# Query and key panels with the weight pieces stationary, and the row scale as a row

## The reference, cut to what matters

```python
hn   = rmsnorm(x, mixer_norm)                       # x * rsqrt(mean(x^2) + eps) * w, per token
proj = hn @ w_in                                    # (256, 2048) @ (2048, 6176)
q, k, v, og, lr = split(proj, 1024, 2048, 4096, 6144)
gk   = lr @ w_gate_up + b_gate                      # lr has rank 2 x 16
logdec = log_sigmoid(gk) / 16
o = gla(q / 16, k, v, logdec) in both directions    # needs q and k with channels down the partitions
o = rmsnorm(o) * silu(og);  x = x + o @ w_out
```

## Time and profile before

| | us |
|---|---|
| median of 3 runs | 1728.8 (1727.99 to 1729.51) |
| span of the profiled execution | 1727.2 |
| PE busy in it | 1705.6 |
| DVE, ACT, POOL busy | 1025.0, 802.1, 99.4 |

### The profile page before, as it was taken

One profiled execution on the slowest core, in us unless ns is written; L12 is line 12 of the kernel. 1 busy time (PEld: TensorE's weight loads), 2 busy tenths in 40 slices (PEclk: granted clock), 3 DMA queues, 4 the chain that ended last, 5 costly groups with the idle time before them and its releaser, 6 DMA issues.

```text
span 1727.2 us, 21748 instructions
## 1 busy us (share of the span) xinstructions
PE 1705.6 (99%) x7827; PEld 1401.8 (81%) x7827; DVE 1025.0 (59%) x1085; ACT 802.1 (46%) x967; POOL 99.4 (6%) x95
## 2 busy tenths in 40 slices
PE   8999999999999999999999999999999999999997
PEld 6888877888777888877888888888888888888886
DVE  4444465566755899955555455455465465565755
ACT  4444444444456555545444443443434444444653
POOL 6000000000110122210000000000000000000001
PEclk9999999999999999999999999999999999999999
DMA  8566645666464644555656566666566666656553
GB/s 258 158 188 184 183 146 147 219 209 215 149 199 134 177 147 152 157 165 180 218 183 190 188 192 191 188 190 191 189 189 191 190 188 192 191 187 194 180 184 133
DMA packets 160175, 315.46 MB, mean 183 GB/s; under 512 B 9772, under 2 KB 11888, under 8 KB 159216
## 3 DMA queue, kind: packets, MB, share of 16 engines
q1 hardware_dynamic: 158480, 304.12, 56.6%
q0 software_dynamic: 1632, 10.46, 1.6%
HBM read 310.36 MB, written 4.19 MB: 182 GB/s over the span
## 4 chain that ended last, share of the span: by engine, by line
PE 96%; DVE 2%; DMA 1%; ACT 1%; issue 0%; POOL 0%; POOLq 0%; DVEq 0%; SPq 0%; ACTq 0%
PE acc L588 29%; PE acc L590 29%; PE acc L589 29%; PE aux L604 2%; PE aux L745 2%; DMA w_raw<-in_w_out 1%; DVE w_lo L1248 1%; PE aux L811 0%; PE aux L637 0%; PE aux L758 0%; PE aux L759 0%; PE aux L636 0%; ACT w_hi L937 0%; DVE h_tok L1478 0%; PE aux L729 0%
## 5 line engine op out<-in xcount | busy, mean ns | idle before, releaser
L1248 DVE TENSOR_TENSOR w_lo<-w_raw,w_hi 128x1024 fp32r<-128x1024 f32 x572 | 704.9, 1236 | 584.7 <-ACT w_hi L937 584.1
L937 ACT CAST w_hi<-w_raw 128x1024 fp32r<-128x1024 f32 x572 | 599.9, 1051 | 821.3 <-PE acc L590 796.6
L588 PE MATMUL acc<-w_hi,a_hi 128*128 128x512 f32 x1664 | 658.6, 396 | 3.0 <-DVE w_lo L1248 3.0
L590 PE MATMUL acc<-w_hi,a_lo 128*128 128x512 f32 x1664 | 650.2, 391 | 0.0
L589 PE MATMUL acc<-w_lo,a_hi 128*128 128x512 f32 x1664 | 649.7, 390 | 0.0
L588 PEld LDWEIGHTS acc<-w_hi,a_hi 128*128 128x128 f32 x1664 | 313.7, 189 | 72.9 <-issue 10.3
L590 PEld LDWEIGHTS acc<-w_hi,a_lo 128*128 128x128 f32 x1664 | 313.4, 188 | 66.5
L589 PEld LDWEIGHTS acc<-w_lo,a_hi 128*128 128x128 f32 x1664 | 313.9, 189 | 62.8 <-issue 0.2
L588 PE MATMUL acc<-w_hi,act_hi 128*128 128x512 f32 x320 | 124.6, 389 | 0.0
L590 PE MATMUL acc<-w_hi,act_lo 128*128 128x512 f32 x320 | 124.5, 389 | 0.0
L589 PE MATMUL acc<-w_lo,act_hi 128*128 128x512 f32 x320 | 124.5, 389 | 0.0
(11 more groups left out here) (236 smaller groups left out, 887.9 us busy)
## 6 DMA issues: line engine op xcount, KB each, us to landing
w_raw<-in_ffn_w_in SPq DMA_DIRECT2D x176, 512.0 KB, 3.4
w_raw<-in_w_in SPq DMA_DIRECT2D x112, 512.0 KB, 3.6
w_raw<-in_gla_w_in SPq DMA_DIRECT2D x96, 512.0 KB, 3.9
w_raw<-in_ffn_w_out SPq DMA_DIRECT2D x88, 512.0 KB, 3.6
w_raw<-in_w_out SPq DMA_DIRECT2D x32, 512.0 KB, 4.7
w_raw<-in_gla_w_out SPq DMA_DIRECT2D x32, 512.0 KB, 3.6
w_raw<-in_ple_w_gate SPq DMA_DIRECT2D x32, 512.0 KB, 3.9
x_tok<-in_x SPq DMA_DIRECT2D x8, 256.0 KB, 8.7
```

The costliest lines, as they stand in the source:

```text
L588: pe.matmul(banks[t][:], hi[:, k + c, tok], wh, start=st, stop=False)
L590: mm = pe.matmul(banks[t][:], lo[:, k + c, tok], wh, start=False, stop=en)
L937: nc.scalar.copy(w_hi[u % RING][:], w_raw[u % RING][:]).then_inc(hi_done, 1)
L1248: nc.vector.tensor_tensor(w_lo[u % RING][:], w_raw[u % RING][:], w_hi[u % RING][:], ALU.subtract).then_inc(lo_done, 1)
```

## The change

In panels 0 to 3 the operands change places. `turned_unit` keeps a piece of the weights, 128 rows by 128 columns, stationary and moves the 256 tokens of `a_hi` or `a_lo` past it: 2 chunks x 4 column blocks x 3 = 24 matmuls of 256 columns. The panel then has output channels down the partitions, as `gqT` and `gkT` want it, so the eight `gt` jobs, the four `stage_panel` calls before them and ACT's copies go; DVE writes `gqT` and `gkT` from the panel's two banks (2 instructions of 128x512 at g = 9, 17, 25, 33).

Tokens now run along the free dimension, so the scale must be a row on all partitions. At g = 6 DVE spreads `rstd[1]` to two 128x128 tiles (`root_wide`), a new job `row` behind unit 7 turns them on PE against the identity (2 float32 matmuls), and ACT copies the result to `root_row` at g = 7. `lr_tok` and `lrt` go as well; DVE scales the rank product with `root_row` at g = 9. The rest of the kernel is the same. The diff, cut:

```diff
@@ gla_jobs
+    if g == 7:
+        found.append(("row", 0))
     if g == 8:
         found.append(("lr", 0))
-    if g in (9, 17, 25, 33):
-        p = (g - 9) // 8
-        found += [("gt", 2 * p), ("gt", 2 * p + 1)]
-    if g == 10:
-        found.append(("lr_tok", 0))
-    if g == 12:
-        found.append(("lrt", 0))
@@ POOL, before the first product with gkT
-                    for i in range(4, 8):
-                        job_read(pool, "gt", i)
+                    panel_read(pool, P_G + 3)
@@ PE
+            def turned_unit(u, p, hi, lo, k, first, last):
+
+                pe.wait_ge(lo_done, u + 1)
+                if first and p >= 2:
+                    panel_read(pe, p - 2)
+                banks = panel_banks(p)
+                for c in range(UNIT):
+                    st, en = first and c == 0, last and c == UNIT - 1
+                    for blk in range(N // P):
+                        half = blk % 2
+                        o = banks[blk // 2][:, half * TOK:(half + 1) * TOK]
+                        wh = w_hi[u % RING][:, c, blk * P:(blk + 1) * P]
+                        wl = w_lo[u % RING][:, c, blk * P:(blk + 1) * P]
+                        pe.matmul(o, wh, hi[:, k + c, :], start=st and half == 0, stop=False)
+                        pe.matmul(o, wh, lo[:, k + c, :], start=False, stop=False)
+                        mm = pe.matmul(o, wl, hi[:, k + c, :], start=False, stop=en and half == 1)
+                mm.then_inc(unit_used, 1)
-                unit(U_G + g, P_G + p, a_hi, a_lo, 2 * j, j == 0, j == UPP - 1)
+                shape = turned_unit if p < 4 else unit
+                shape(U_G + g, P_G + p, a_hi, a_lo, 2 * j, j == 0, j == UPP - 1)
...
+                    if name == "row":
+
+                        pe.wait_ge(root_spread, TT)
+                        b = begin("row")
                         for t in range(TT):
+                            mm = pe.matmul(b[:, t * P:(t + 1) * P], root_wide[:, t, :], ident[:], start=True, stop=True)
...
                     if name == "dg":
                         if i == 0:
-                            job_read(pe, "gt", 6)
-                            job_read(pe, "gt", 7)
+                            panel_read(pe, P_G + 3)
@@ ACT (the copies of lr, lr_tok, lrt and gt go too)
+                if g == 7:
+                    job_done(act, "row")
+                    nc.scalar.copy(root_row[:], bank_of("row")[:, 0:TOK]).then_inc(read_of("row"), 1)
...
-                    if p < 4:
+                    if 4 <= p < 8:
                         act.wait_ge(rstd_done, 2)
-                        stage_panel(P_G + p, og[p % 2], rstd[1])
@@ DVE, behind low(U_G + g + RING)
-                    nc.vector.memset(lrt[:, :, 2 * RANK:], 1.0).then_inc(zeros, 1)
+                    nc.vector.memset(lrT[2 * RANK:2 * RANK + 1, :], 1.0).then_inc(zeros, 1)
...
+                if g == 6:
+                    dve.wait_ge(rstd_done, 2)
+                    for t in range(TT):
+                        nc.vector.tensor_scalar(root_wide[:, t, :], ident[:], 0.0, rstd[1][:, t:t + 1], ALU.mult,
+                                                ALU.add).then_inc(root_spread, 1)
+                if g == 9:
+                    job_read(dve, "row")
+                    job_done(dve, "lr")
+                    nc.vector.tensor_tensor(lrT[0:2 * RANK, :], bank_of("lr")[0:2 * RANK, 0:TOK],
+                                            root_row[0:2 * RANK, :], ALU.mult).then_inc(read_of("lr"), 1)
+                if g in (9, 17, 25, 33):
+                    p = (g - 9) // 8
+                    panel_done(dve, P_G + p)
+                    row = root_row[:].rearrange("p (a t) -> p a t", a=1).broadcast_to([P, 2, TOK])
+                    for i, b in enumerate(panel_banks(P_G + p)):
+                        src = b[:].rearrange("p (k t) -> p k t", t=TOK)
+                        k = 4 * (p % 2) + 2 * i
+                        nc.vector.scalar_tensor_tensor((gqT if p < 2 else gkT)[:, k:k + 2, :], src,
+                                                       1.0 / 16.0 if p < 2 else 1.0, row, ALU.mult,
+                                                       ALU.mult).then_inc(acc_read[(P_G + p) % 2], 1)
```

More of the change, by code:

```diff
@@ L240, in block_kernel @@
     lr_lo = at("lr_lo", [P, KD, 2 * RANK], F32R, W + 60 * KB)
-    lrt = at("lrt", [P, TT, 2 * RANK + 1], F32, W + 64 * KB)
+    root_row = at("root_row", [P, TOK], F32, W + 62 * KB)
+    root_wide = at("root_wide", [P, TT, P], F32, W + 63 * KB)
     lrT = at("lrT", [2 * RANK + 1, TOK], F32, W + 64 * KB + 288)
@@ L324, in block_kernel @@
         fg_split, lr_split = sem("fg_split"), sem("lr_split")
+        root_spread = sem("root_spread")
         tanh_done = sem("tanh_done")
@@ L785, in _ @@
                         thin("lr", lr_hi, lr_lo, 2 * RANK)
[L786 to L793, removed]
-                        for t in range(TT):
[L795 to L802, removed]
+                    if name == "row":
+                        pe.wait_ge(root_spread, TT)
+                        b = begin("row")
+                        for t in range(TT):
+                            mm = pe.matmul(b[:, t * P:(t + 1) * P], root_wide[:, t, :], ident[:], start=True, stop=True)
                         mm.then_inc(aux_done, 1)
@@ L805, in _ @@
                         if i == 0:
-                            job_read(pe, "lrt")
+                            job_read(pe, "lr")
                             pe.wait_ge(up_in, 64)
@@ L1144, in _ @@
                 if j == UPP - 1:
-                    if p < 4:
+                    if 4 <= p < 8:
                         act.wait_ge(rstd_done, 2)
-                        stage_panel(P_G + p, og[p % 2], rstd[1])
-                    elif p < 8:
                         act.wait_ge(emb_out, 16)
                         stage_panel(P_G + p, gv[:, :, (p - 4) * N:(p - 3) * N], rstd[1])
-                    else:
+                    elif p >= 8:
                         if p >= 10:
@@ L1529, in times @@
                 if s == 0:
-                    for i in range(4):
-                        job_read(dve, "gt", i)
+                    panel_read(dve, P_G + 1)
                 d = decayed[2 * (s % 2) + 1]
```

## The result

| | before | after |
|---|---|---|
| median, us (4 runs each) | 1728.5 (1727.99 to 1729.51) | 1738.9 (1738.33 to 1740.02) |
| span of the profiled execution | 1727.2 | 1736.6 |
| PE busy | 1705.6 | 1707.9 |

The changed kernel is slower: ratio 1.0062, 95% interval 1.0050 to 1.0074, or 10.4 us. The forecast was 1736.6 in a range of 1732.0 to 1741.0. On the page, PE's busy time hardly moves against the earlier trace rows, while the span grows by 9.4: most of the loss, 7.1 us, is PE not working.

What follows compares the result with a forecast made beforehand. The prediction took PE, busy 99% of the span, to bound the kernel. Its terms, 0.7 - 2.4 + 5.65 + 1.4 + 1.5 + 1.0 = +7.8 us, gave 1736.6 us, range 1732.0 to 1741.0.

Steps and rivals of the forecast that it cites:

- Bound: Whole kernel: PE, busy for 99% of the span; what it does or waits for is the time.
- The wait in front of unit 8: Behind unit 7, `row` waits for DVE's spread tiles; with the job +5.65 us, bounds 5.0 to 6.2.
- The clock behind it: After the wait before unit 8, PE runs 3.41 us at half speed: +1.4 us, bounds 0.5 to 2.4.
- The pace of turned units: Units 8 to 24: 256-column matmuls 0.115 us apart, 0.04 more per unit, +0.7 us; bounds 0.1 to 1.9.
- Removed jobs: PE ahead of the key panels: `gt` pairs at g = 9 and 17, `lr_tok` and `lrt` go, -2.4 us.
- The key copy: Before `dg`, PE waits for DVE's `gkT` at g = 33: +1.5 us, plus +1.0 for a lower clock.
- At no cost: ACT's changed copies, DVE's other added instructions and POOL's first `gkT` product 1.5 us later add no time.
- Rival 1: Before unit 8: the spread is in time and the kernel gets faster, -2.8 us, 1726.0; chance 0.05.
- Rival 2: Only the wait before unit 8 costs; key copy hides, clock stays up at `dg`: +3.6 us, 1732.4; chance 0.11.
- Rival 3: Turned units: full-width loads set the pace; chance 0.04 for non-overlapping loads or a fixed part per pair, 0.1 for contention.
- mild form: Turned units: some load contention, 0.122 us a matmul, +3.5 us, about 1739.5; chance 0.1.
- heavy form: Turned units: loads cannot overlap, 0.19 us each, 4.5 a unit, +57 us, 1793; chance 0.04, shared with a fixed part per pair.

Runs made afterwards that it cites:

- row_late: Changed kernel with the job `row` moved from behind unit 7 to behind unit 10, its DVE readers moved along, spread unchanged: 1732.7 us, ratio 1.0022.
- both_narrow: As both, with the turned units' stationary pieces 32 columns wide instead of 128, leaving out three quarters of queries and keys: 1724.1 us, ratio 0.9973.
- both: Changed kernel with `row` moved behind unit 10 and DVE's second key-half copy moved to the start of g = 32: 1728.8 us, ratio 1.0000.
- both_flat: As both, with the old unit of 512-column matmuls in panels 0 to 3, queries and keys left unturned: 1724.9 us, ratio 0.9975.
- key_early: Changed kernel with DVE copying the second key half at the start of g = 32 instead of at g = 33: 1736.2 us, ratio 1.0047.
- both_swap: As both, with each block's three products reordered so no stationary piece is loaded twice in a row: 1728.5 us, ratio 0.9995.
- both_round: As both, with the three products going round the four column blocks so neighbouring matmuls write to different places: 1728.4 us, ratio 0.9999.
- both_96: As both, with stationary pieces 96 columns wide, leaving out a quarter of queries and keys: 1727.5 us in a single run.

## Why the prediction came out right, point by point

- *Bound.* PE's chain and its waits decide. Confirmed: removing two PE waits gave back 10.1 of the 10.4 us.
- *The wait in front of unit 8*, +5.65 with the job. The shape was exact: DVE serves two residues first, and PE idles 4.84 us. Unit 8 is 5.98 us later against unit 7 than it was. The spread was faster than its nearest row made it, 0.47 for both against 0.55, and the job from its first matmul to unit 8 took 0.88 (all of it at the lower clock) against 0.65.
- *The clock behind it*, +1.4 with bounds 0.5 to 2.4. Measured 2.4, the upper bound: the half-clock level lasted 6.83 us, not one stretch of 3.41, and covered `row` and unit 8 but for its last matmuls (10.57 against 8.17 for unit 8 and `lr`). Of this 0.16 is the pace: against row_late, 8.33, the clock costs 2.2 on unit 8, and 0.44 more on the job. The step that failed in size is the one that took the length of the stretch from a single case behind a 2 us idle time.
- *The pace of turned units*, +0.7 for 17 units from 0.115. Measured 0.120, so 17 x 0.16 = 2.7. This is the term that was most mis-sized, and it came out above the bound of 1.9. The 0.115 was read from a level step whose matmuls are float32 with 128 moving columns; there each load meets another kind of matmul. The two rows that I combined (loads of full width at 0.115, float32r matmuls at 0.114 with loads of 32) did not show the combination, and it is 5 ns worse than either. That `lr` row was also the quick one of two: the product 8 wide goes at 0.117. Why full loads cost 5 ns is not shown; both_narrow shows only that narrow ones can do without.
- *Removed jobs*, -2.4 for those ahead of the keys. By the unit intervals, with 0.16 (0.13 where a `gk` job stands in both) put in for the pace, units 9 to 13 and 17 give -2.5. Right.
- *The key copy*, +1.5 and +1.0 for the clock. Measured from unit 25 to 35: +3.13, with a wait of 2.39 where 3.05 was forecast. PE came later than I had it, by the same pace error, and DVE's two instructions took 1.28, not 1.5. The clock fell, which the forecast had left open, and stayed low for 3.41 us, of which 2.98 fell on `dg`: 1.5.
- *At no cost.* Right: DVE's load at g = 25, ACT's loss of work and POOL's later start show in no wait of PE, and the distances behind unit 35 are those of before to 0.02 us.
- *Rival 1* (faster) fails on its own condition: the spread came 4.5 us behind unit 7. The run with both moves is its world in effect, at no change instead of the -2.8 that was worked out; the difference is mostly the pace, which both_flat puts at 3.9. *Rival 2* was wrong in that the key copy did not hide. *Rival 3* in its mild form (0.122) was closer to the pace than the forecast's own 0.115; its heavy form is refuted by 0.120. So is the fixed part per pair that the rule of the Trainium skill (TensorE: Matmul & The Clock Gate, Back-to-back issue gap) would give here: a turned unit is 0.16 us longer than an old one, not the 0.78 worked out from that rule. Its direction, that more and shorter pairs cost something, was right.

The sum of the forecast's terms was 7.8. With the measured sizes it is 2.7 - 2.5 + 6.0 + 2.4 + 3.1 = 11.7; the ledger shows 9.46 + 1.80 = 11.3 between unit 7 and unit 35. The 0.4 between them is unit 8's own 0.16, which is in the pace and in its stretched interval, and 0.03 for each of eight units with a `gk` job.

So the mechanism was right in all its parts and most sizes were too small in the same direction: 7.8 was forecast where 11.3 came. The range held them, since its upper bound allowed for terms like these. That the time came within 2.3 us of the forecast is partly luck: the medians differ by 0.9 less than the ledger, probably through the half-clock stretches that the changed kernel's runs were spared.

## What to carry to other kernels

Before work is taken off the bounding engine, look at when its replacement's input is made, on which engine's queue, and how many instructions stand ahead of it there: here a job standing ahead of its input and a copy standing behind two residues cost 10 us, all of the loss; putting the job three units later and the copy ahead of both residues cost nothing. An idle time of a few microseconds on TensorE is to be priced with the lower clock behind it, which added 2.7 us to 4.8 and 1.5 to 2.4 here. And swapping operands so that a matmul halves its columns doubles its loads; read the distance of exactly that pair of load and matmul, not of each alone, and at more than one place of the trace.

## What the runs showed of the hardware

- With stationary pieces 128 wide, float32r matmuls of 256 columns start 0.120 us apart in every turned unit at the full clock (after, row_late, key_early, both), whichever piece is loaded (both_swap) and wherever they write (both_round). Two of them cost 0.240, one of 512 columns 0.227.
- With narrower pieces the pace differs from place to place within one run: 0.113, 0.118 or 0.120 with 32 columns (both_narrow), 0.116 in the mean with 96 (both_96), 0.117 with 8 (before).
- After an idle time of 4.84 us TensorE was at the 1.2 GHz level for 6.83 us, in 5.81 of which it was busy; after 2.0 (before, unit 4) and 2.4 us (after, `dg`) for 3.41 us.
- Half-clock stretches came at the same place in some profiles and not in others. In unit 4 before, row_late and both have one, after and key_early none, with the same 5.42 us from unit 3 to unit 4 in front of it. It is worth 1.5 us, and the one ahead of unit 0 about as much, so a difference of up to 3 us between two single profiles need not be a change's.
